# Second layer of a diffusion backbone: routing and gathered experts in one stage, head by head, with the sums over v on TensorE

## What is computed

```
def peer_ffn(h, w_q, keys, u, v):          # h: tokens x 1024
    q = (xb @ w_q).reshape(T, 8, 2, 128)
    s = jnp.einsum('thpd,hpnd->thpn', q, keys)          # two halves of 128 sub-keys
    s_top, i_top = lax.top_k(s, 16)
    cand = s_top[:, :, 0, :, None] + s_top[:, :, 1, None, :]      # 256 candidates
    cidx = i_top[:, :, 0, :, None] * 128 + i_top[:, :, 1, None, :]
    best, sel = lax.top_k(cand, 16)
    eidx = jnp.take_along_axis(cidx, sel, axis=-1)
    g = jax.nn.softmax(best, axis=-1)
    act = jax.nn.gelu(jnp.einsum('td,thkd->thk', xb, u[eidx]))
    return jnp.einsum('thk,thkd->td', g * act, v[eidx])
x = rms_norm(x + mod * peer_ffn(...), final_norm_g)     # the end of the second layer
```

## Time and profile before

| | us |
|---|---|
| three runs: median (lowest to highest) | 3504.57 (3502.87 to 3515.21) |
| the profiled execution: device time | 3521.81 |
| the profiled execution: span of the profile | 3520.0 |
| in it: routing of layer 2 | 2605 to 2737 |
| in it: gathered experts of layer 2 | 2737 to 3501 |
| in it: final norm and store | 3501 to 3520 |

### The profile page before, as it was taken

The page is one execution under the profiler, slowest core; times in us unless marked ns, Lnnn a source line. Parts: engine busy times, 40 slices in busy tenths (PEclk is TensorE's granted clock), DMA queues, the critical chain, the costliest instruction groups (busy, mean ns, idle before and its releaser), DMA issues. The chain is left out here.

```text
span 3520.0 us, 39566 instructions
## 1 busy us (share of the span) xinstructions
PE 2081.6 (59%) x14514; PEld 1722.2 (49%) x14514; DVE 2339.6 (66%) x4625; ACT 872.1 (25%) x1497; POOL 1453.4 (41%) x1267
## 2 busy tenths in 40 slices
PE   4967797795667778788999996946763000000000
PEld 2847644593457767677777775835563000000000
DVE  2267646289968988887433334284539886988967
ACT  2222244221362333333333333222431000000000
POOL 0004200230026765564645540022042677777774
PEclk7975688896798998998999998956886555555555
DMA  4230003133359999999999992200030899999995
GB/s 173 81 123 1 8 1 129 64 109 144 144 238 384 400 399 344 399 393 386 404 400 400 402 375 84 67 1 8 1 128 28 302 379 387 328 346 368 378 393 184
DMA packets 265515, 816.61 MB, mean 232 GB/s; under 512 B 26672, under 2 KB 62064, under 8 KB 263920
## 3 DMA queue, kind: packets, MB, share of 16 engines
q0 software_dynamic: 147456, 536.94, 39.8%
q1 hardware_dynamic: 117872, 277.21, 21.5%
HBM read 796.22 MB, written 17.83 MB: 231 GB/s over the span
## 5 line engine op out<-in xcount | busy, mean ns | idle before, releaser
L1660 PE MATMUL ps<-ident,sparse_acc 128*128 128x128 f32 x16 | 3.9, 428 | 754.1 <-DVE sparse_acc L1694 754.1
L1825 POOL DMA_INDIRECT sparse_ring<-in_v_rows,eidT x256 | 278.2, 1087 | 320.8 <-PE ps L1874 246.8
L1825 POOL DMA_INDIRECT sparse_ring<-in_u_rows,eid x256 | 347.0, 1355 | 122.1 <-issue 68.1
L1694 DVE SCALAR_TENSOR_TENSOR sparse_acc<-sparse_v,sparse_wt,sparse_acc 128x1024 f32<-128x1024 f32 x256 | 329.1, 1286 | 87.9 <-remote 44.4
L116 PE MATMUL ps<-h_hi,peer_uh 128*128 128x256 f32 x1024 | 313.3, 306 | 110.4 <-DVE peer_ul L1937 101.3
L1660 PEld LDWEIGHTS ps<-ident,sparse_acc 128*128 128x128 f32 x16 | 3.1, 224 | 754.9 <-DVE sparse_acc L1694 754.9
L1636 POOL DMA_INDIRECT sparse_u<-in_u_rows,eid x256 | 286.0, 1117 | 147.5 <-issue 78.3
L1937 DVE TENSOR_TENSOR peer_ul<-peer_u,peer_uh 128x1024 fp32r<-128x1024 f32 x128 | 156.5, 1223 | 275.5 <-ACT peer_uh L1902 202.9
L1684 DVE CUSTOM_DVE_ANT_0 sparse_u<-sparse_u,sparse_h 128x1024 f32<-128x1024 f32 x256 | 313.4, 1224 | 34.9 <-DMA sparse_u<-in_u_rows,eid 32.7
L1644 POOL DMA_INDIRECT sparse_v<-in_v_rows,eid x256 | 294.9, 1152 | 81.5 <-issue 73.7
L1963 DVE CUSTOM_DVE_ANT_0 sparse_ring<-sparse_ring,hT 128x1024 f32<-128x1024 f32 x256 | 304.0, 1223 | 36.7 <-DMA sparse_ring<-in_u_rows,eid 31.8
(11 more groups left out here) (340 smaller groups left out, 5664.2 us busy)
## 6 DMA issues: line engine op xcount, KB each, us to landing
peer_u<-in_uT SPq DMA_DIRECT2D x128, 512.0 KB
peer_v<-in_v_rows SPq DMA_DIRECT2D x128, 512.0 KB
ada_slab<-in_ada_w SPq DMA_DIRECT2D x24, 2048.0 KB, 8.2
proj_slab<-in_w_fm SPq DMA_DIRECT2D x38, 512.0 KB
route_slab<-in_w_pq SPq DMA_DIRECT2D x32, 512.0 KB, 3.6
peer_gates<-dense_stage SPq DMA_DIRECT2D x8, 2048.0 KB
peer_gates<-peer_gates SPq DMA_DIRECT2D x32, 512.0 KB
out_slab<-in_w_out SPq DMA_DIRECT2D x16, 512.0 KB, 3.7
```

The costliest lines, as they stand in the source:

```text
L1694: nc.vector.scalar_tensor_tensor(out=acc[:, r // NS], in0=vb[:, r % RV], scalar=wt[:, r:r + 1], in1=acc[:, r // NS], op0=ALU.mult, op1=ALU ...
L1825: nc.gpsimd.indirect_dma_start(out=ring[:, s % R], out_offset=None, in_=rows, in_offset=bass.IndirectOffsetOnAxis(ap=at, axis=0)).then_inc ...
```

## The change

`phase_route` and `phase_sparse` of the last layer become one stage, `phase_stream`. The first layer is untouched.

- `hT` is made in `phase_norm` (its argument `turned`), and after that stage the semaphores are cleared behind an all-engine barrier (`clear_layer_sems`).
- VectorE routes one head of one tile at a time (`route(t, h)`), down to the expert numbers of that head, and marks `eid_done`. `top16` runs over the two halves of one tile. The scores of all 16 half-heads are kept (`s_sb` has 16 slots).
- GpSimd issues the 16 u gathers of a head of tile 0 behind `eid_done`. Its subtractions for `wl` stand between them: four before, two ahead of each of the first six heads.
- u and v rows share one ring of 18 slots, in the order of the list `order`: u of tile 0; 32 v of tile 0; 8 times (16 u of tile 1, 12 v of tile 0); 128 v of tile 1. A v gather serves one token, as in the first layer.
- The sum over v is on TensorE in quads; a v slot is free when the quad that reads it is through. VectorE has no more `scalar_tensor_tensor` over v.
- VectorE's order: routes of tile 0 with the dots of the head before in between; the last dots; `route(1, 0)`; the weights of tile 0 and their spread into `wdiag`; the routes and dots of tile 1; weights, `add_back(0)`, spread, `add_back(1)`.

```diff
-        def phase_sparse(l, lo, h2, eid, gate):
+        def phase_stream(l, lo, hp, hT):
-            RU, RV = 12, 12
+            R = 18
+            AHEAD = 32
+            SHARE = (P - AHEAD) // PH
+
+            order = [("u", 0, s) for s in range(NS)] + [("v", 0, o) for o in range(AHEAD)]
+            for h in range(PH):
+                order += [("u", 1, TOPK * h + k) for k in range(TOPK)]
+                order += [("v", 0, o) for o in range(AHEAD + SHARE * h, AHEAD + SHARE * (h + 1))]
+            order += [("v", 1, o) for o in range(P)]
...
+            def consumed(s):
+
+                kind, t, i = order[s]
+                if kind == "u":
+                    return dot_done, dots_upto[s + 1]
+                return quad_mm, 32 * t + i // 4 + 1
...
                     def _(pool):
-                        for g in range(NGR + LAG):
-                            for j in range(GS):
-                                    nc.gpsimd.indirect_dma_start(
-                                        out=ub[:, r % RU], out_offset=None, in_=d["u_rows"],
-                                        in_offset=bass.IndirectOffsetOnAxis(ap=eid[:, r // NS, r % NS:r % NS + 1], axis=0)
-                                    nc.gpsimd.indirect_dma_start(
-                                        out=vb[:, r % RV], out_offset=None, in_=d["v_rows"],
-                                        in_offset=bass.IndirectOffsetOnAxis(ap=eid[:, r // NS, r % NS:r % NS + 1], axis=0)
-                                    ).then_inc(v_in[r % RV], 16)
+                        for c in range(4):
+                            low(c)
+                        nc.gpsimd.memset(wdiag[:], 0.0).then_inc(diag_cleared, 1)
+                        for s, (kind, t, i) in enumerate(order):
+                            if kind == "u" and t == 0 and i % TOPK == 0:
+                                for c in range(2 * (i // TOPK) + 4, min(2 * (i // TOPK) + 6, HP)):
+                                    low(c)
+                            if s >= R:
+                                pool.wait_ge(*consumed(s - R))
+                            if kind == "u":
+                                if i % TOPK == 0:
+                                    pool.wait_ge(eid_done, PH * t + i // TOPK + 1)
+                                rows, col = d["u_rows"], eid[:, t, i:i + 1]
+                            else:
+                                if i == 0:
+                                    pool.wait_ge(eidT_ev, t + 1)
+                                token = 32 * (i % 4) + i // 4
+                                rows, col = d["v_rows"], eidT[:, t, token:token + 1]
+                            nc.gpsimd.indirect_dma_start(out=ring[:, s % R], out_offset=None, in_=rows,
+                                                         in_offset=bass.IndirectOffsetOnAxis(ap=col, axis=0)).then_inc(row_in[s % R], 16)
...
-                            pe.wait_ge(acc_done, NS * (t + 1))
+                        def quad(t, j):
+
+                            if j == 0:
+                                pe.wait_ge(spread, t + 1)
+                                if t:
+                                    pe.wait_ge(acc_ev, 2 * t)
+                            slots = [at["v", t, 4 * j + q] for q in range(4)]
+                            for s in slots:
+                                pe.wait_ge(row_in[s % R], 16 * (s // R + 1))
+                            for half in range(2):
+                                for q, s in enumerate(slots):
+                                    mm = nc.tensor.matmul(ps[32 * q:32 * (q + 1), 6 + half, :], wdiag[:, q, j, :],
+                                                          ring[:, s % R, half * BANK:(half + 1) * BANK], start=(j == 0), stop=(j == 31))
+                            mm.then_inc(quad_mm, 1)
...
+                        sub_scores(HP - 1)
+                        turn_eid(0)
+                        turn_weights(0)
+                        for j in range(32):
+                            if j == 28:
+                                turn_eid(1)
+                            quad(0, j)
+                        pe.wait_ge(s_ev, HP)
+                        turn_back(0)
+                        turn_weights(1)
+                        for j in range(32):
+                            quad(1, j)
+                        turn_back(1)
...
-                                    nc.vector.tensor_tensor_reduce(
-                                        out=ub[:, r % RU], in0=ub[:, r % RU], in1=hT[:, r // NS], scale=1.0, scalar=0.0,
-                                        op0=ALU.mult, op1=ALU.add, accum_out=dots[:, r:r + 1]).then_inc(dot_done, 1)
-                                    nc.vector.scalar_tensor_tensor(out=acc[:, r // NS], in0=vb[:, r % RV], scalar=wt[:, r:r + 1],
-                                                                   in1=acc[:, r // NS], op0=ALU.mult, op1=ALU.add).then_inc(acc_done, 1)
...
+                        def route(t, h):
+
+                            dve.wait_ge(s_ev, 2 * h + 2)
+                            step(top16(lambda k: top[:, k], lambda k: idx[:, k], lambda k: s_sb[:, 2 * h + k, t], lambda k: s2[:, k], 2))
+                            nc.vector.tensor_copy(idf[:], idx[:])
+                            step(nc.vector.tensor_tensor(cand[:], bc(top[:, 0], 2, TOPK), bc(top[:, 1], 1, TOPK), ALU.add))
+                            step(top16(lambda k: best[:, t, h], lambda k: sel[:], lambda k: cand[:].rearrange("p a b -> p (a b)"),
+                                       lambda k: cand2[:], 1))
+                            nc.vector.tensor_scalar(sela[:, 0], sel[:], 4, None, ALU.logical_shift_right)
+                            step(nc.vector.tensor_scalar(sela[:, 1], sel[:], 15, None, ALU.bitwise_and))
+                            step(nc.vector.tensor_copy(self_[:], sela[:].rearrange("p j k -> p (j k)")))
+                            step(nc.vector.tensor_tensor(eq[:], bc(self_[:], 2, TOPK), bc(iota[:, 0:TOPK], 1, 2 * TOPK), ALU.is_equal))
+                            e4 = eq[:].rearrange("p (j k) a -> p j k a", j=2)
+                            step(nc.vector.tensor_tensor(e4, e4, bc(idf[:], 2, TOPK), ALU.mult))
+                            step(nc.vector.tensor_reduce(ij[:].rearrange("p j k -> p (j k)"), eq[:], AX, ALU.add))
+                            step(nc.vector.scalar_tensor_tensor(out=ij[:, 0], in0=ij[:, 0], scalar=float(NKEY), in1=ij[:, 1],
+                                                                op0=ALU.mult, op1=ALU.add))
+                            cols = slice(TOPK * h, TOPK * (h + 1))
+                            nc.vector.tensor_scalar(eidf[:, t, cols], ij[:, 0], float(l * NKEY * NKEY), None, ALU.add)
+                            nc.vector.tensor_scalar(eid[:, t, cols], ij[:, 0], float(l * NKEY * NKEY), None, ALU.add).then_inc(eid_done, 1)
...
+                        def dot(t, h):
+
+                            for i in range(TOPK * h, TOPK * (h + 1)):
+                                s = at["u", t, i]
+                                dve.wait_ge(row_in[s % R], 16 * (s // R + 1))
+                                nc.vector.tensor_tensor_reduce(
+                                    out=ring[:, s % R], in0=ring[:, s % R], in1=hT[:, t], scale=1.0, scalar=0.0,
+                                    op0=ALU.mult, op1=ALU.add, accum_out=dots[:, t, i:i + 1]).then_inc(dot_done, 1)
...
+                        def spread_weights(t):
+                            dve.wait_ge(wt_mm, t + 1)
+                            dve.wait_ge(diag_cleared, 1)
+                            if t:
+                                dve.wait_ge(quad_mm, 32 * t)
+                            nc.vector.tensor_copy(diag, ps[:, 4, P:2 * P].rearrange("p (q j) -> p q j", q=4)).then_inc(spread, 1)
...
+                        for h in range(PH):
+                            route(0, h)
+                            if h == PH - 1:
+                                softmax_arg(0)
+                            if h:
+                                dot(0, h - 1)
+                        turned_ids(0)
+                        softmax(0)
+                        dot(0, PH - 1)
+                        route(1, 0)
+                        weights(0)
+                        spread_weights(0)
+                        for h in range(1, PH):
+                            route(1, h)
+                            if h == PH - 1:
+                                softmax_arg(1)
+                            dot(1, h - 1)
+                        turned_ids(1)
+                        softmax(1)
+                        dot(1, PH - 1)
+                        weights(1)
+                        add_back(0)
+                        spread_weights(1)
+                        add_back(1)
...
-                eid, eidT = (sb(st, f"{x}{l}", [P, nt, PH * TOPK], U32) for x in ("eid", "eidT"))
-                gate = sb(st, f"gate{l}", [P, nt, PH * TOPK])
```

(10 more changed lines are left out.)

229 lines of the change are left out of this document (164 added, 65 removed).

## The result

The changed kernel takes 3474.9 us (median of four runs, 3468.9 to 3480.4), the kernel before 3509.4 (four runs). The ratio is 0.990, 95% interval 0.987 to 0.993: 34.5 us or 1.0% faster. The prediction was 3388, range 3355 to 3440. The direction was right; two thirds of the gain is missing, and the range did not hold the time.

The account below looks back on a forecast made before the run. Bound: routing set by VectorE with nothing gathered, then gathering set by DMA engines and GpSimd's issue. Start -103, gathers with hole -6 and end -7 make -116.4 us, from 3504.6 to 3388 us; range 3355 to 3440.

Parts of the forecast that it names:

- the start: Ahead of the gathers: norm, semaphore clearing and one route put the first gather near 2636, 103 us earlier.
- the end: From the last gather's issue to the stage's last add: 11.1 us instead of 18.3, worth -7 us.
- the first tile: Tile 0's routes, dots and 128 gathers: VectorE ends at 2859, GpSimd about 2843, so VectorE sets this phase.
- from there 6 times: VectorE's head cycles in tile 0: route 8.5, 16 dots 18.4, port contention 2; 173 us for six, to 2838.9.
- the first tile is slower: Rival, chance 0.2: each head's cycle takes 35 us instead of 28.9, second tile's gathers 1.45 us; total 3436 us.
- the hole: GpSimd stands 13 us from 2860, as the 19th v row needs a quad whose weights stand behind `route(1, 0)`.
- the pace of the gathers: The 366 gathers after the hole: 238 at 1.405 us beside VectorE's work, 128 at 1.30; last issue at 3373.
- 128 v rows go beside an idle VectorE: 1.30, 166 us: Tile 1's 128 v gathers, last in the stage, take 1.30 us each, 166 us in all.
- that is the bound from the bytes: A gather's 524,288 bytes at the best window's 404 GB/s take 1.30 us; 512 gathers take 666 us.
- -6 for the gathers: Term for the gathers with their hole: first to last issue 738 us instead of 744.
- The rival in which dots do not slow the issue: Chance 0.15: 238 gathers beside VectorE's work take 1.30 us instead of 1.405, 25 us less, total 3363 us.

Follow-up runs that it names:

- run 29: Not a run's label: in "lets the gathers run 29 us ahead of 1.40 each", "run" is a verb and 29 us a time.

## Why the prediction came out wrong

**Right: the start.** 103 us forecast, 102.0 by the rows once the drift ahead of the norm is taken off. The norm and the clearing are 1.0 us longer than before, where 1.3 was allowed. The first route takes 9.6 us, the others of the first tile 8.5 to 8.9, where 8.5 was summed from the earlier trace rows.

**Right: the end.** 11.1 us forecast from the last issue to the last add, 12.2 measured (3444.31 to 3456.50). That is two errors that partly cancel: the last quad starts 5.7 us behind the last issue instead of 3.6, and takes 2.46 us instead of 3.64, at a granted clock of 0.86 (3447 to 3453) where 0.50 was priced. The adds are as summed.

**Wrong size: the first tile (+31 us).** The step was "from there 6 times 28.9 us". The cycle was 31.8 us, so VectorE's last dot came 21 us late, at 2888.1, and GpSimd, which I had 16 us ahead of VectorE, was only 5 us ahead, about the time that a row takes to land: it set the end of the tile as much as VectorE did. I had the 1.99 us gathers' row (1.86 in the earlier trace rows) and the subtractions' contention, and priced the two at 2 us a head. The run without the subtractions shows 23 us for them. The rival "the first tile is slower" had the right mechanism at twice the size (6 us a head), with a chance of 0.2.

**Half wrong: the hole.** Thirteen us of standing near 2860 were forecast; GpSimd waited 2.8 us, at 2908. Its last u gather of the tile began at 2881.4, so its own issue had taken the time instead. The prediction said that the hole would close in that case.

**Wrong: the pace of the gathers (+14 and +17 us).** The step that failed is "128 v rows go beside an idle VectorE: 1.30, 166 us", and behind it "that is the bound from the bytes". I took the best window of 40 us, 404 GB/s, as a price that can be had for as long as one likes. It is lent: 1.24 us a gather for a stretch, 1.40 to 1.46 for every kernel over 128 gathers. The rows to doubt it were there: the earlier trace rows has 382 and 341 GB/s with the DMA engines at 1.00 and 0.94, and the earlier trace rows make 743.1 us for 511 steps, 1.454 each. I explained that average by VectorE's two operations a row and so let it fall when one of them went. Without either, it is still 1.44. The 256 scaled adds that left VectorE bought at most the 7.5 us of the run that routes first, and with them fell the "-6 for the gathers".

**The range.** It had the slower first tile in it, but no case in which the mean pace of before stayed: the 384 gathers behind the first tile at 1.454 us are 558 us (measured 560.7) where 530 were forecast. That alone gives 3416, and with the slower first tile's 37 us 3453, above the range. The rival in which dots do not slow the issue went the wrong way: half of the first tile's u gathers beside dots take about 2.0 us.

**What stays open.** What serves one gather in 1.40 us. The runs exclude the ring, TensorE's work and reads, VectorE, the bytes, the data packets and the DMA engines' share; what is left goes by the gather or by what every gather has alike (128 indices, 16 small packets), lets the gathers run 29 us ahead of 1.40 each when all else rests, and meanwhile signals of other engines come late (12 us after a quad's modelled end above; up to 20 us with 28 slots, by the semaphore events of that trace). With all engines at work GpSimd stops after 16 to 40. That the signals and TensorE's products are held by the same thing is argued from their going together and from the 1.40 us in both, not shown.

The Trainium skill, page "NOTIFIC — the notification-queue block", section "7.1 Overflow: three behaviours, one of which stalls the engine", says that the block which writes the trace's records holds its producers back rather than lose a record inside. If that is the limit, a part of it belongs to the recording. The records of DMA packets would not set it by their number, since 144 and 80 packets a gather end at the same 1.40 us. All runs here, timed ones too, come with a span and a granted clock of their own, so none can tell; no run here shows it.

## What to carry to other kernels

Price a long run of transfers by the mean of the longest stretch that the trace has, never by its best window, and ask what else could explain that mean before you let it fall. When a wait's releaser is named, change the resource it stands for (here the ring, from 14 to 28 slots) before you believe it: a wait can be the paying back of a debt. An engine that helps at the seams of another's work (subtractions between gathers) costs what it delays in both; an idle engine that does it in a dearer way can be the better buy.

## What the runs showed of the hardware

- A gather of 128 rows took GpSimd 0.94 us and 0.30 to the next, 410 GB/s, for 146 in a row with all other engines at rest; then 1.10 and 0.30, with rows of 4 KB and of 2 KB alike (128 and 64 data packets of 4,096 bytes), each time 29 us ahead of 1.40 us a gather. The transfers themselves went on at 1.28 us a gather.
- While gathers ran at 1.24 us, products of a quad whose rows had landed started 1.40 us apart (28 slots).
- Over 128 gathers at the end of the stage, 15 kernels with 14 to 28 slots, 8 or 16 products a quad and issues of 1.24 to 1.46 us took 181 to 186 us.
- After a run at 1.24 us GpSimd, waiting for a quad's signal, stood for 0.18 to 0.2 us per gather of the run (0.15 to 0.17 with half rows).
- Two subtractions of 128x1024 operands in a row on GpSimd (4.67 us) stretched a dot on VectorE that had begun just before them from 1.23 to 5.87 us; another pair, meeting two dots, took 5.84 us, and the dots 3.4 each.
- A gather of u rows beside dots took 0.94 or up to 1.99 us, 1.58 on average in the first tile; beside an idle VectorE always 0.94.
- The DMA engines' busy share was 0.97 at 360 GB/s and 1.03 at 410, so the share does not tell a free engine from a full one.
